# Moving an expert-output gate from the final sum into each expert's rows, with a per-tile end

## What is computed

```python
h = rms_norm(x, g_ffn) * (1.0 + sc2) + sh2
x = x + gt2 * moe_ffn(h, ...)          # gt2: one factor for each of the 1024 columns
return rms_norm(x, g_final)

# moe_ffn: top 4 of 32 experts for each token, softmax over the four logits
ys  = ((up + 1.0) * glu) @ w_down[e] + b_down[e]     # rows of one expert
out = segment_sum(ys * row_w, row_tok)               # summed back to the tokens
```

## Time and profile before

| | |
|---|---|
| median of three runs | 2197.66 us |
| all three | 2198.87, 2193.72, 2197.66 us |
| the profiled execution | 2200.27 us |
| its span, first to last instruction | 2198.5 us |
| mean granted TensorE clock | 0.965 |
| PE, DVE, ACT, POOL busy | 93%, 28%, 14%, 3% of the span |
| DMA | 599.8 MB, 273 GB/s mean |

### The profile page before, as it was taken

The page is one execution under the profiler, slowest core; times in us unless marked ns, Lnnn a source line. Parts: engine busy times, 40 slices in busy tenths (PEclk is TensorE's granted clock), DMA queues, the critical chain, the costliest instruction groups (busy, mean ns, idle before and its releaser), DMA issues.

```text
span 2198.5 us, 24406 instructions
## 1 busy us (share of the span) xinstructions
PE 2054.9 (93%) x9982; PEld 1171.2 (53%) x9982; DVE 608.1 (28%) x1191; ACT 316.1 (14%) x703; POOL 65.0 (3%) x68
## 2 busy tenths in 40 slices
PE   8988999999998999999778999999999999999996
PEld 7766688847766678846634333333333333333332
DVE  0467453312367430004632111111111111111112
ACT  1324110001324210002420000000000000000001
POOL 0022000000022000000010000000000000000000
PEclk9989999999979999999886999999999999999999
DMA  7430078864320045444107999999999999999995
GB/s 296 153 116 1 1 283 303 344 229 171 144 96 31 20 165 228 153 166 153 48 7 290 409 428 429 428 428 429 429 428 428 429 428 429 429 428 427 429 428 252
DMA packets 43823, 599.77 MB, mean 273 GB/s; under 512 B 4992, under 2 KB 5296, under 8 KB 7888
## 3 DMA queue, kind: packets, MB, share of 16 engines
q1 hardware_dynamic: 43760, 598.87, 66.5%
HBM read 597.78 MB, written 1.07 MB: 272 GB/s over the span
## 4 chain that ended last, share of the span: by engine, by line
PE 68%; DMA 22%; DVE 7%; ACT 1%; issue 1%; SPq 0%; DVEq 0%; ACTq 0%
DMA ring<-in_stream 22%; PE ps L1821 14%; PE ps L1234 14%; PE ps L1255 7%; PE ps L376 6%; PE ps L1848 3%; PE ps L390 2%; PE ps L1161 2%; PE ps L1803 2%; PE ps L1898 2%; PE ps L1810 2%; PE ps L1586 1%; PE ps L777 1%; PE ps L789 1%; DVE SB L762 1%
## 5 line engine op out<-in xcount | busy, mean ns | idle before, releaser
L1821 PE MATMUL ps<-ring,HT 128*64 128x512 f32 x2176 | 488.8, 599 | 11.0 <-DMA ring<-in_stream 11.0
L1821 PEld LDWEIGHTS ps<-ring,HT 128*64 128x64 f32 x2176 | 147.9, 137 | 326.5 <-issue 277.1
L1234 PE MATMUL ps<-XT,ring 128*128 128x256 f32 (+1 forms) x1536 | 306.0, 362 | 3.3 <-DVE XT L313 3.3
L1234 PEld LDWEIGHTS ps<-XT,ring 128*128 128x128 f32 x1536 | 271.9, 190 | 36.8 <-DVE XT L313 3.7
L1848 PE MATMUL ps<-ring,HT 128*64 128x512 f32 x1088 | 248.0, 598 | 33.7 <-DMA ring<-in_stream 32.8
L1848 PEld LDWEIGHTS ps<-ring,HT 128*64 128x64 f32 x1088 | 72.6, 136 | 196.1 <-issue 121.3
L1255 PE MATMUL ps<-ring,HT 128*128 128x512 f32 x352 | 151.7, 592 | 0.0
L376 PE MATMUL ps<-XT,ring 128*128 128x256 f32 x576 | 126.6, 383 | 1.3 <-DMA ring<-in_stream 1.3
L1956 DVE TENSOR_SCALAR HT<-ps 128x512 f32<-128x512 f32 x34 | 23.5, 692 | 350.3 <-PE ps L1821 350.3
L376 PEld LDWEIGHTS ps<-XT,ring 128*128 128x128 f32 x576 | 110.7, 192 | 17.0 <-issue 1.7
L1255 PEld LDWEIGHTS ps<-ring,HT 128*128 128x128 f32 x352 | 66.7, 190 | 82.4 <-issue 82.3
(11 more groups left out here) (394 smaller groups left out, 1841.0 us busy)
## 6 DMA issues: line engine op xcount, KB each, us to landing
ring<-in_stream SPq DMA_DIRECT2D x278, 2048.0 KB, 14.6
SB<-in_ln SPq DMA_DIRECT2D x8, 512.0 KB, 9.6
SB<-mod_rows SPq DMA_DIRECT2D x1, 3072.0 KB, 9.8
CST<-in_const SPq DMA_DIRECT2D x1, 1362.0 KB, 5.4
PAR<-in_layer SPq DMA_DIRECT2D x2, 558.5 KB, 11.2
X<-in_x SPq DMA_DIRECT2D x1, 1024.0 KB, 4.9
HN<-in_head_norm SPq DMA_DIRECT2D x2, 512.0 KB, 12.1
SB<-in_gains SPq DMA_DIRECT2D x2, 512.0 KB, 9.8
```

The lines of the kernel that those rows point to most:

```text
L1234: m = pe.matmul(ps[:, 2 * (f % 2) + a, j * T + cols.start:j * T + cols.stop], w[:, k, a, j * P:(j + 1) * P], XT[:, k, cols], start=k == 0, ...
L1821: m = pe.matmul(ps[HD * half:HD * (half + 1), a, :], XE[:, 2 * b + k, q * SLOTS_E:(q + 1) * SLOTS_E], w[:, k, a, half, :], start=False, st ...
```

## The change

Every use of the gate `MOD[:, 5]` at the end is moved forward, and three details of the end are changed with it.

- POOL gets two more instructions behind `modulated_pool`: the second half of the gate row is copied over the first half on partitions 64 to 127 (64 x 512), so that it fits the layout of `EY`; and the 32 bias rows `BD` are multiplied by the gate (32 x 1024). Before them it waits for `x_ready`, `h_rows` and `par2_loaded`. Both signal `h_rows`.
- PE's wait ahead of the bias matmuls is now for `h_rows` at 6 instead of `par2_loaded` at 64. DVE waits once, ahead of its loop, for `h_rows` at 5.
- `moe_rows_dve` multiplies by the gate instead of copying.
- The last return signals `moe_done` once for each tile, and the extra transpose goes; the `moe_sc` signal, which nothing waits for, goes too.
- `final_dve` only adds, each tile after its own signal.
- ACT calls `root_table_act` behind the last Sigmoid.
- SP stores each tile by itself, 512 KB each.

```diff
+        def gated_pool(pool):
+
+            pool.wait_ge(S("x_ready"), 2 * DEPTH + 1)
+            pool.wait_ge(S("h_rows"), 2 * NT)
+            nc.gpsimd.tensor_copy(MOD[HD:P, 5, 0:512], MOD[HD:P, 5, 512:1024]).then_inc(S("h_rows"), 1)
+            pool.wait_ge(S("par2_loaded"), 64)
+            pool.wait_ge(S("h_rows"), 2 * NT + 1)
+            nc.gpsimd.tensor_tensor(BD[0:NE, :], BD[0:NE, :], MOD[0:NE, 5, :], ALU.mult).then_inc(S("h_rows"), 1)
...
-            pe.wait_ge(S("par2_loaded"), 64)
+            pe.wait_ge(S("h_rows"), 2 * NT + 2)
             for t in range(NT):
                 for c in range(2):
                     pe.matmul(ps[:, 4 + 2 * t + c, :], GTT[0:NE, t * P:(t + 1) * P], BD[0:NE, c * 512:(c + 1) * 512],
...
             pe.wait_ge(S("moe_y_evac"), last * 2 + 3)
-            moe_return_pe(pe)
-            pe.transpose(ps[:, 0, 0:P], ident, ident).then_inc(S("moe_done"), 1)
-
-        def moe_return_pe(pe):
+            moe_return_pe(pe, True)
+
+        def moe_return_pe(pe, end=False):
 
             for t in range(NT):
                 for c in range(2):
                     rows = slice(HD * c, HD * (c + 1))
                     m = pe.matmul(ps[:, 4 + 2 * t + c, :], EPT[rows, t * P:(t + 1) * P], EY[rows, :],
                                   start=False, stop=True, skip_group_check=True)
-            m.then_inc(S("moe_sc"), 1)
+                if end:
+                    m.then_inc(S("moe_done"), 1)
...
             moe_sigmoid_act(act, last * 2 + 2)
+            root_table_act(act)
             moe_turn_act(act, last, 1)
...
             v.wait_ge(S("moe_slot"), used)
-            nc.vector.tensor_copy(EY, ps[:, 3, :]).then_inc(S("moe_y_evac"), 1)
+            nc.vector.tensor_tensor(EY, ps[:, 3, :], MOD[:, 5, 0:512], ALU.mult).then_inc(S("moe_y_evac"), 1)
...
             moe_hidden_dve(v, RING + AHEAD, 1)
+            v.wait_ge(S("h_rows"), 2 * NT + 1)
             with v.Fori(0, last) as it:
...
-            v.wait_ge(S("moe_done"), 1)
-            for t in range(NT):
-                L(nc.vector.tensor_tensor(YT, bank(4 + 2 * t, 2), MOD[:, 5, :], ALU.mult))
-                nc.vector.tensor_tensor(X[:, t, :], X[:, t, :], YT, ALU.add).then_inc(S("x_tile" if t == 0 else "x_ready"), 1)
-                v.wait_ge(S("x_tile" if t == 0 else "x_ready"), 2 * DEPTH + 2)
+            for t in range(NT):
+                v.wait_ge(S("moe_done"), t + 1)
+                nc.vector.tensor_tensor(X[:, t, :], X[:, t, :], bank(4 + 2 * t, 2), ALU.add
+                                        ).then_inc(S("x_tile" if t == 0 else "x_ready"), 1)
...
-            sp.wait_ge(S("final"), NT)
-            sp.dma_start(dram["out"].rearrange("(t p) d -> p t d", p=P), X[:]).then_inc(S("stored"), 16)
-            sp.wait_ge(S("stored"), 16)
+            for t in range(NT):
+                sp.wait_ge(S("final"), t + 1)
+                sp.dma_start(dram["out"][t * P:(t + 1) * P, :], X[:, t, :]).then_inc(S("stored"), 16)
+            sp.wait_ge(S("stored"), 16 * NT)
...
             for t in range(NT):
                 modulated_pool(pool, t)
+            gated_pool(pool)
```

## The result

The changed kernel takes 2188.43 us (median of 20 runs, 2184.87 to 2197.98), the kernel before 2198.19 us in the same comparison (20 runs, 2191.83 to 2203.81). The ratio is 0.9961, with a 95% interval from 0.9951 to 0.9972: faster by 0.39%, or 8.6 us on the means. The prediction was 2193.9 in a range from 2190.0 to 2198.5. The direction was right, the gain is about twice the one forecast, and the time lies 1.6 us under the range.

The account below looks back on a forecast made before the run. The expert loop was taken to be bound by DMA's weight stream, the router and tail by serial chains. Tail gain 4.75 less POOL's stall 1.0 gives 3.75 us: 2197.66 to 2193.9, range 2190.0 to 2198.5.

Parts of the forecast that it names:

- Its own sign of being wrong: Behind the router: the forecast is wrong if the windows from 1170 to 1250 show another clock.
- The loop at no cost: In the expert loop, the copy turned multiply, the dropped signal and DVE's new wait cost nothing.
- The tail, 4.75: From the last return to the end: 3.65 us from earlier, fewer DVE operations plus 1.1 from the store, 4.75 gained.
- The store: At the kernel's end, two 512 KB stores landing in 2.9 us each gain 1.1 us; bounds 0 to 1.9.
- The preload as cover for 1.28 us: In the tail, the table load moved behind the last Sigmoid costs nothing; without that cover it costs 1.28 us.
- Rival 2: In the tail, Copy and Square take the preloaded table away: Sqrt 1.0 us later, gain 2.75, 2194.9; chance 0.07.
- POOL's stall, 1.0: In the router, POOL's multiply holds DVE's L1686 until it ends: 1.0 us lost, bounds 0 to 1.3.
- Rival 1: In the router, POOL's two instructions disturb nothing: gain 4.75 us, 2192.9; chance 0.15.
- A slow-down in proportion: In the router, POOL stretches five or six DVE operations by a fifth, some 0.2 us; the sum 0.8 better.
- PE kept waiting by POOL: At the bias matmuls, PE arrives 9.7 us after POOL's multiply ends, so the new wait costs nothing.
- rivals 3 and 4: Clock from 1170: 3, PE loses 3.4 us twice, 2200.7, chance 0.12; 4, the dip goes, 2190.5, chance 0.13.
- rival 4: In the expert stream, the 6.8 us half-clock dip is gone: 3.4 us more gained, 2190.5; chance 0.13.

Follow-up runs that it names:

- e6: Changed kernel with the single 1 MB store of before: ratio 0.9983 to the kernel before, tail 11.87 us.
- e5: Changed kernel without the preload of the root table: ratio 0.9986 to the kernel before, tail 11.51 us.
- e3: Kernel before plus POOL's two instructions alone, writing to a row that nothing reads: ratio 1.0005 to the kernel before.
- e4: Changed kernel with POOL's copy of the gate row moved ahead of the modulated rows: ratio 0.9986 to the kernel before.
- e8: Kernel before with signal per tile, store per tile and preload, gate still multiplied at the end: ratio 0.9989 to the kernel before.
- e10: Changed kernel with four more linked DVE operations (1.0 us) in the router: ratio 0.9974 to the kernel before.
- e9: Kernel before with seven more linked DVE operations (some 1.75 us) in the router: ratio 1.0002 to the kernel before.
- e1: Kernel before once more, unchanged, timed against itself: ratio 1.0002.
- e14: Kernel before a third time, unchanged, timed against itself: ratio 0.9999.
- e7: Changed kernel with one signal after the extra transpose for both tiles, as before: ratio 0.9988 to the kernel before, tail 11.58 us.

## Why the prediction was wrong in size, and where it was right

The terms that it added up were right within 0.5 us in all. What it put at nothing in its sum, the granted clock, is where the rest of the measured difference lies. Its own sign of being wrong came true: the windows from 1170 to 1250 show another clock.

**The loop at no cost**: right. 34 multiplies in 0.69 each, and neither new wait was waited for.

**The tail, 4.75**: right, 5.02. The first add came 1.17 behind the return's start (1.15 forecast), L1380 3.68 behind it (3.67 forecast, 7.32 before). The store gained 1.4 instead of 1.1 (e6). Of these 0.3 us 0.2 are that 512 KB land in 2.7 and not 2.9; the straight line between 128 KB and 1 MB was a little pessimistic.

**The preload as cover for 1.28 us**: right, 1.03 when taken away. Rival 2 falls: no load stands at L1374 in the changed trace. With the load in the chain (e5), the Sqrt started 1.30 behind the load's start. The Trainium skill gives 2.66 us for each switch, page "ScalarE: Activation LUTs", section "What ACT_TABLE_LOAD costs"; e5 disagrees, as the row in the prediction did, and the measurement decides.

**POOL's stall, 1.0**: right in kind, 0.81 in size. The copy took 0.61 and not 1.0, while the gaps around it were 0.13 and 0.15 and not 0.08; the multiply took 2.33. It was L1683 that was held and not L1686, which I had named second. By the same rule of overlap less 0.14: 1156.40 - 1155.44 - 0.14 = 0.82. That POOL's two instructions cause it alone is shown by e3 and e4. Rival 1 falls. A slow-down in proportion doesn't fit, since 0.17 became 0.98. The Trainium skill describes a lock in "SBUF — State Buffer" (section "Who interferes with whom"), and by it a tensor_scalar whose input and output are in SBUF can contend as well as an operation with two SBUF inputs. These figures agree with it.

**PE kept waiting by POOL**: right that it isn't.

**The step that failed is the clock, as rivals 3 and 4 had it.** I put the clock at nothing in the sum, took its two outcomes as equally likely luck, 0.12 and 0.13, and ended the range at the good one. But rival 4, the vanished stretch, came, and in the first comparison more besides: 7.5 of the 11.7 us between the two profiled executions lie ahead of the change and in the stream. Three things were wrong in that step.

First, the stretch is not symmetrical luck. I wrote that all engines are shifted together, and that is so among themselves; against the clock they are not. The stall of 0.8 us that I had booked as a loss is what moves one of the alignments out of the stretch: at 37.49 the four traces with it (the changed kernel twice, e5, e6) have no stretch, and the one without it (e8) has. Across the 14 traces without idle-time matmuls, the stretch is present in all seven in which the rise comes 12.5 to 13.3 behind the first load, and absent in all six in which it comes 11.3 to 11.7 (the fourteenth is e10). The stream takes 1012.8 us on the mean with it and 1010.5 without: it is worth 2.3 us, not rival 4's 3.4. That the ring of four slots gives the rest back is my reading and was not tested. The kernel before had it in two traces of three, the changed one and its three variants with the same router in two of six. So the change gains perhaps 1 us here on the mean (2.3 x 1/3 = 0.8), an estimate from few traces. e9 supports the mechanism with one trace, and e10 shows its limit; neither shows this mean. That the first trace of the changed kernel was the one without the stretch was luck in part.

Second, the clock ahead of the change is no constant. L1410 starts between 1136.7 and 1150.9 in the traces, with the same code ahead of it. In eleven traces the clock is at half for 6.8 or 13.7 us at about 240 or 742, where PE is the busy engine, and there L1410 starts at 1144.3 on the mean; in the seven without, at 1138.9. A single profiled execution carries this. The value that I started from, 2197.66, was not at fault: the mean of all 177 executions of the kernel before is 2197.76.

Third, the size. In all sessions together the changed kernel (44 executions) lies 6.9 us below the one before (177 executions, e1 and e14 with them), standard error 0.6; session by session 8.6, 4.9 and 7.4. The parts that are shown come to 4.2, with the stretch to about 5. What is left, some 2 us, stays open. It is not in the tail or the router, whose times repeat within 0.02 us. In the traces it lies ahead of the change: twelve traces of the changed kernel and its variants start L1410 at 1140.8 on the mean, six of the kernel before and its variants at 1145.1, in code that is the same. The half clock at 240 or 742 is in all six of the kernel before and its variants and in five of the twelve others. The mean granted clock, recorded for each execution, points the same way: 0.9640 on the mean of 157 executions of the kernel before (those of the four sessions) and 0.9663 of the 44 of the changed one, of which the shorter tail, 5.0 us less at about 0.64, makes some 0.0007 by my estimate. So what is left goes with the clock; what gives the changed kernel more of it is not shown. The variants speak with two voices. e4 to e7, corrected by what they undo, show nothing of it (5.0, 3.2, 2.8 and 3.1 expected from the fixed parts, 3.2, 4.0, 4.2 and 2.65 measured); e10 does (3.2 expected, 5.7 measured, standard error 1.0). Whether the spread of executions or something in the loaded program makes this I can't say.

## What to carry to other kernels

Work off the bound engine is worth moving into an operation that runs anyway (a copy became a multiply at the same 0.69 us), if what has to be prepared for it is checked for what it holds up on DVE: two POOL operations of together 2.9 us, which nothing waits for until 10.8 us later, put 0.8 us on the critical chain, because a two-column DVE operation was held until the second of them ended. At the end of this kernel each tile's own signal gained 1.1 us and its own store 1.4. Where the forecast gain is as small as the kernel's spread from the clock, count that spread into the range, in both directions, and read several executions of both kernels before calling any of it luck.

## What the runs showed of the hardware that was not expected

- The end of the router's half clock stood at a few fixed distances from L1410 (38.35, 37.49, once 36.3 us), and by theory D 0.8 us of stall in one of these alignments decided on 6.8 us of half clock more than 40 us later. Adding 1.8 us of work to the kernel before gave the ratio 1.0002 (0.9986 to 1.0017), which would not exclude 1.8 us, while its stream was 1.9 to 3.8 us shorter than in the two traces of that kernel that have the stretch.
- PE kept busy with matmuls that nothing reads brought the logits from 6.9 to 3.8 us and the changed kernel to 0.9951 and 0.9956 of the time before. Beside the changed kernel itself this is 2.8 us (standard error 1.3), and it is not part of the change.
- A negation of 128 x 2 on DVE was held by a POOL multiply from 0.17 to 0.98 us, while a PSUM read with one SBUF operand (0.22) and a top-8 (0.29) beside the same multiply were not held.
- POOL's copy of 64 x 512 took 0.61 us, half of an add of the same columns (1.27). The multiply of 32 partitions x 1024 took 2.33, as long as one of 128 partitions (2.35).
